# The last expert layer's end: gate multiplied into the down weights, the second tile summed by TensorE, the output stored in halves

## The reference

```python
def post_norm(x, y, gate, g, b):
    return layer_norm(DEEPNORM_ALPHA * x + gate * y, g, b)
...
    combine = jnp.sum(jax.nn.one_hot(e_idx, N_EXPERTS, dtype=jnp.float32) * wts[..., None], -2)
    hid = jax.nn.silu(jnp.einsum('bld,edf->blef', h, w_gate)) * jnp.einsum('bld,edf->blef', h, w_up)
    y = jnp.einsum('blef,efd->bld', hid * combine[..., None].astype(hid.dtype), w_down)
...
        x = post_norm(x, moe(modulate(x, ml[3], ml[4]), w_router, b_router, w_gate[i], w_up[i], w_down[i]),
                      ml[5], ln_g[i, 1], ln_b[i, 1])
```

## Time and profile before

| what | value |
|---|---|
| median of 3 runs | 901.22 us (898.92 to 905.03) |
| the profiled execution | 900.66 us |
| its span in the trace | 898.8 us |
| TensorE busy | 740.8 us (82% of the span) |
| VectorE busy | 477.4 us (53%) |
| DMA share and rate, 825 to 850 us | 1.02, 404 GB/s |
| TensorE busy from 870 us to the end | 0 us |

### The profile page before, as it was taken

One profiled execution on the slowest core, in us unless ns is written; L12 is line 12 of the kernel. 1 busy time (PEld: TensorE's weight loads), 2 busy tenths in 40 slices (PEclk: granted clock), 3 DMA queues, 4 the chain that ended last, 5 costly groups with the idle time before them and its releaser, 6 DMA issues. The chain is left out here.

```text
span 898.8 us, 15497 instructions
## 1 busy us (share of the span) xinstructions
PE 740.8 (82%) x5225; PEld 431.1 (48%) x5225; DVE 477.4 (53%) x1089; ACT 316.9 (35%) x778; POOL 300.1 (33%) x702
## 2 busy tenths in 40 slices
PE   0988879999997177999999999999898547999950
PEld 0544435555553023556666566665655233555520
DVE  1048654533334583643767777777744753443326
ACT  0240322222222225644657566575641121222211
POOL 0000113443344000366164846648440012434330
PEclk9989969999999569995999999999997857999985
DMA  9999999999990899576152442522110299999912
GB/s 250 408 394 393 411 412 406 408 408 346 359 390 25 326 367 261 186 205 209 41 145 52 108 124 53 142 60 100 43 60 1 104 403 392 404 405 407 376 65 112
DMA packets 107239, 219.34 MB, mean 244 GB/s; under 512 B 28293, under 2 KB 63437, under 8 KB 102817
## 3 DMA queue, kind: packets, MB, share of 16 engines
q1 hardware_dynamic: 98207, 200.39, 61.9%
q0 software_dynamic: 8224, 15.76, 4.6%
q10 hardware_dynamic: 740, 2.32, 0.9%
HBM read 212.09 MB, written 17.33 MB: 255 GB/s over the span
## 5 line engine op out<-in xcount | busy, mean ns | idle before, releaser
L1234 PE MATMUL banks<-h_cols,weight_ring 128*128 128x512 f32 (+1 forms) x384 | 160.3, 538 | 0.7
L1211 POOL TENSOR_TENSOR arena<-arena 128x60 f32<-128x60 f32 (+24 forms) x248 | 81.8, 330 | 123.3 <-DMA arena<-blocks 104.5
L1213 POOL TENSOR_TENSOR arena<-arena 128x60 f32<-128x60 f32 (+24 forms) x248 | 84.0, 339 | 19.4
L903 POOL DMA_INDIRECT y_of_tokens<-arena,place_now x42 | 47.3, 1126 | 127.9 <-ACT arena L795 127.9
L747 PE MATMUL banks<-arena 128*64 128x512 f32 x352 | 85.2, 605 | 3.0 <-DVE arena L839 3.0
L1234 PEld LDWEIGHTS banks<-h_cols,weight_ring 128*128 128x128 f32 x384 | 66.2, 194 | 34.7 <-issue 31.7
L875 POOL DMA_INDIRECT arena<-h_of_tokens,row_now x50 | 53.1, 1063 | 80.7 <-DVE token_of_slot L715 35.3
L287 PE MATMUL banks<-weight_ring,c_cols 128*32 128x512 f32 x368 | 52.3, 687 | 29.3 <-DMA weight_ring<-in_w_mod_dram 29.3
L765 PE MATMUL banks<-weight_ring,arena 128*64 128x256 f32 x576 | 67.6, 388 | 0.9 <-DVE arena L827 0.9
L831 DVE TENSOR_TENSOR arena<-arena,banks 128x128 f32<-128x128 f32 x42 | 12.1, 288 | 102.8 <-ACT arena L800 102.8
L800 ACT ACTIVATE arena<-banks 128x128 f32<-128x128 f32 x42 | 11.7, 278 | 143.1 <-PE banks L765 143.1
(11 more groups left out here) (291 smaller groups left out, 1374.7 us busy)
## 6 DMA issues: line engine op xcount, KB each, us to landing
weight_ring<-in_w_mod_dram SPq DMA_DIRECT2D x46, 1024.0 KB, 9.9
weight_ring<-in_dn_w_in_dram SPq DMA_DIRECT2D x32, 512.0 KB, 7.0
weight_ring<-in_w_gate_dram SPq DMA_DIRECT2D x13, 1024.0 KB, 10.5
weight_ring<-in_w_up_dram SPq DMA_DIRECT2D x13, 1024.0 KB, 14.6
weight_ring<-in_w_down_dram SPq DMA_DIRECT2D x13, 1024.0 KB, 15.5
arena<-in_w_gate_dram SPq DMA_DIRECT2D x7, 1024.0 KB, 12.5
arena<-in_w_up_dram SPq DMA_DIRECT2D x7, 1024.0 KB, 14.6
arena<-in_w_down_dram SPq DMA_DIRECT2D x7, 1024.0 KB, 16.3
```

Source lines behind the costliest of these rows:

```text
L903: pool.indirect_dma_start(y_halves, bass.IndirectOffsetOnAxis(m.place_now[:, u:u + 1], 0), v.y_tile[u], None, bounds_check=last_row, oob_i ...
L1211: then(pool.tensor_tensor(part, U[:, 0:q, j:j + 1].to_broadcast([P, q, BLK - 1 - j]), M[:, j, j + 1:BLK].unsqueeze(1).to_broadcast([P, q, ...
L1213: ins = pool.tensor_tensor(U[:, 0:q, j + 1:BLK], U[:, 0:q, j + 1:BLK], part, ALU.subtract)
L1234: mm = pe.matmul(bank(6 + j % 2)[:, 0:CTX + SEQ - n0], head_w[h % 2][:, j, k, :], m.hT[:, k, n0:CTX + SEQ], start=(k == 0), stop=(k == KD ...
```

## The change

- In the second layer, L839's copy becomes a product: `down_now` = down weights times the gate vector. In the first layer it stays a copy.
- Behind experts 2 and 3 VectorE multiplies one tile of x by ALPHA, in place; behind expert 4 it makes two diagonal matrices of 128 x 128 with the second tile's two weights (`weight_diag`).
- In GpSimd's loop (`pair`, in both layers) the wait for the earlier y store and the `place_now` copy stand first, ahead of `row_now` and the fetch of rows.
- Behind the last `down()` TensorE puts the second tile's x into banks 3 and 4 by a product with the identity (2 calls), makes 12 products into bank 1 that nobody reads, waits for the second tile's y and adds both pieces through the diagonals (4 calls).
- VectorE sums the first tile in two instructions instead of three, takes the second tile from the banks, and makes the last pass in halves of 512 columns. ScalarE no longer scales y.
- SyncE stores each half when it is done: four stores of 256 KB instead of two of 512 KB.

```diff
@@ dve_moe, tile
                 for to, of in down_pieces(expert_slot(L, e)):
-                    ins = dve.tensor_copy(to, of)
+                    if L.n == 0:
+                        ins = dve.tensor_copy(to, of)
+                    else:
+                        to, of = (x.rearrange("p (c n) -> p c n", n=D) for x in (to, of))
+                        ins = dve.tensor_tensor(to, of, mod_vec(GATE2).unsqueeze(1).to_broadcast([P, to.shape[1], D]), ALU.mult)
                 ins.then_inc(s(t_ + "hidden"), 1)
@@ dve_moe, behind expert e
+                if L.n == 1 and 2 <= e < 2 + XT:
+                    dve.wait_ge(s("ln_x"), MT + 2 * XT)
+                    x = m.x[:, L.x_tiles[e - 2], :]
+                    dve.tensor_scalar(x, x, ALPHA, None, ALU.mult).then_inc(s("x_scaled"), 1)
+                if L.n == 1 and e == 2 + XT:
+                    for c in range(2):
+                        dve.tensor_scalar(weight_diag[c], v.ident, v.weights[:, c, 1:2], None, ALU.mult).then_inc(s("x_scaled"), 1)
@@ pool_moe, pair
                 for u in range(2):
+                    if not first:
+                        pool.wait_ge(s(t_ + f"y_stored{u}"), 16 * j - 16)
+                    pool.tensor_copy(m.place_now[:, u:u + 1], m.place_of[:, bass.ds(2 * j + u - 2, 1)]
+                                     ).then_inc(s(t_ + f"place_now{u}"), 1)
                     pool.wait_ge(s(t_ + "rows_copied"), 2 * j + u + 1)
...
                     rows(u, u)
-                    if not first:
-                        pool.wait_ge(s(t_ + f"y_stored{u}"), 16 * j - 16)
-                    pool.tensor_copy(m.place_now[:, u:u + 1], m.place_of[:, bass.ds(2 * j + u - 2, 1)]
-                                     ).then_inc(s(t_ + f"place_now{u}"), 1)
@@ new
+        def pe_last_sum(pe):
+            t = XT - 1
+            pe.wait_ge(s("x_scaled"), XT + 2)
+            for half in range(2):
+                pe.matmul(m.ps[:, 3 + half, :], v.ident, m.x[:, L1.x_tiles[t], half * BANK:(half + 1) * BANK], start=True, stop=False)
+            for n in range(12):
+                pe.matmul(m.ps[:, 1, :], v.ident, m.const[:, 0:BANK], start=True, stop=True)
+            pe.wait_ge(s(f"y_back{t % 2}"), 32 * 3)
+            for c in range(2):
+                for half in range(2):
+                    mm = pe.matmul(m.ps[:, 3 + half, :], weight_diag[c], v.back[:, t, c, half * BANK:(half + 1) * BANK],
+                                   start=False, stop=(c == 1))
+            mm.then_inc(s("y_mixed"), 1)
+
+        def dve_last_norm(dve, t):
...
+            if t < XT - 1:
+                dve.wait_ge(s("x_scaled"), XT)
+                dve.wait_ge(s(f"y_back{t % 2}"), 32 * 3)
+                dve.scalar_tensor_tensor(out=x, in0=v.back[:, t, 0, :], scalar=v.weights[:, 0, t:t + 1], in1=x, op0=ALU.mult,
+                                         op1=ALU.add).then_inc(s("ln_gated"), 1)
+                dve.wait_ge(s("ln_gated"), c + 1)
+                dve.scalar_tensor_tensor(out=x, in0=v.back[:, t, 1, :], scalar=v.weights[:, 1, t:t + 1], in1=x, op0=ALU.mult,
+                                         op1=ALU.add).then_inc(s("ln_summed"), 1)
+                dve.wait_ge(s("ln_summed"), c + 1)
+            else:
+                dve.wait_ge(s("y_mixed"), MT + 1)
+                x = last_sum()
@@ sync
             for n, t in enumerate(L1.x_tiles):
-                sp.wait_ge(s("ln_x"), MT + 2 * XT + n + 1)
-                sp.dma_start(out_dram[0, n * P:(n + 1) * P, :], m.x[:, t, :]).then_inc(s("stored"), 16)
-            sp.wait_ge(s("stored"), 16 * XT)
+                for half in range(2):
+                    cols = slice(half * BANK, (half + 1) * BANK)
+                    sp.wait_ge(s("ln_x"), MT + 2 * XT + 2 * n + half + 1)
+                    sp.dma_start(out_dram[0, n * P:(n + 1) * P, cols], m.x[:, t, cols]).then_inc(s("stored"), 16)
+            sp.wait_ge(s("stored"), 16 * XT * 2)
@@ tensor
             pe_moe(pe, L1)
+            pe_last_sum(pe)
```

More of the change, by code:

```diff
@@ L924, in sp_back, with last_sum @@
                     sp.dma_start(v.back[:, t, c, :], y_dram[row:row + P, :]).then_inc(s(f"y_back{t % 2}"), 16)
+        weight_diag = [m.c_cols.rearrange("p k n -> p (k n)")[:, c * P:(c + 1) * P] for c in range(2)]
+        def last_sum():
+            return m.ps[:, 3:5, :].rearrange("p a n -> p (a n)")
+        def pe_last_sum(pe):
[11 more added lines that the diff above has]
+            mm.then_inc(s("y_mixed"), 1)
@@ new lines, in dve_last_norm @@
+        def dve_last_norm(dve, t):
+            c = LN_BASE["ln1b_"] + t
+            x = m.x[:, L1.x_tiles[t], :]
+            if t < XT - 1:
[11 more added lines that the diff above has]
+            for half in range(2):
+                dve.bn_stats(v.stats[:, 2 * (t % 2) + half, :], x[:, half * BANK:(half + 1) * BANK]).then_inc(s("ln_stats"), 1)
+            dve.wait_ge(s("ln_stats"), 2 * c + 2)
+            dve.bn_aggr(v.mean_var[:, t, 0:2], v.stats[:, 2 * (t % 2):2 * (t % 2) + 2, :]).then_inc(s("ln_var"), 1)
@@ new lines, in dve_last_centred @@
+        def dve_last_centred(dve, t):
+            c = LN_BASE["ln1b_"] + t
+            x = m.x[:, L1.x_tiles[t], :]
+            dve.wait_ge(s("ln_var"), c + 1)
+            dve.scalar_tensor_tensor(out=x, in0=x if t < XT - 1 else last_sum(), scalar=v.mean_var[:, t, 0:1], in1=m.ln[:, 0, :],
+                                     op0=ALU.subtract, op1=ALU.mult).then_inc(s("ln_centred"), 1)
+            dve.wait_ge(s("ln_std"), c + 1)
+            dve.reciprocal(v.mean_var[:, t, 2:3], v.std[:, t:t + 1]).then_inc(s("ln_rstd"), 1)
@@ L926, in act_back, with dve_last_scaled @@
+        def dve_last_scaled(dve, t, half):
+            c = LN_BASE["ln1b_"] + t
+            cols = slice(half * BANK, (half + 1) * BANK)
+            x = m.x[:, L1.x_tiles[t], cols]
+            dve.wait_ge(s("ln_centred"), c + 1)
+            dve.wait_ge(s("ln_rstd"), c + 1)
+            dve.scalar_tensor_tensor(out=x, in0=x, scalar=v.mean_var[:, t, 2:3], in1=m.ln[:, 1, cols], op0=ALU.mult, op1=ALU.add
+                                     ).then_inc(s("ln_x"), 1)
         def act_back(act, L, t):
@@ L2200, in _ @@
             act_moe(act, L1)
-            act_moe_norms(act, L1, "ln1b_")
+            for t in range(XT):
+                act_std(act, "ln1b_", t)
         @block.tensor
@@ L2328, in _ @@
             for t in range(XT):
[L2329 to L2332, removed]
+                dve_last_norm(dve, t)
+                dve_last_centred(dve, t)
+                for half in range(2):
+                    dve_last_scaled(dve, t, half)
 def constants():
```

## The result

The changed kernel takes 897.06 us (median of 9 runs, 894.75 to 899.06), the one before 901.53 us (9 runs, 898.92 to 907.34): ratio 0.9941, 95% interval 0.9917 to 0.9965. By the medians that is 4.5 us less, or 0.5%; by the ratio it is 0.6%, 5.3 us. 893.5 was forecast, 7.7 us less. The profiled execution has a span of 897.2 us; at 899.06 us it is the longest of the nine.

What follows compares the result with a forecast made beforehand. Bound: TensorE in the loop, then the chain from last down product to last store. 0.04 + 5.95 + 0.65 at the end plus 1.1 in the first layer make 7.7 us less: 893.5 us, range 890.5 to 897.5.

Steps and rivals of the forecast that it cites:

- (b): Rival: TensorE's clock falls in the longer gap before the last down product, +2 to +3.5 us, 896 us; chance 0.08.
- The product: Second layer's loop, VectorE: down weights times gate take 2.30 us against the copy's 1.22, 1.08 us more per tile.
- Its cover in the loop: The 1.08 us fit VectorE's idle time before L831 (2.50, tightest 1.18) and cost nothing, except at the last tile.
- VectorE's two tiles: End of the kernel: first tile 7.01 us instead of 8.07, second 4.45 us; together with the earlier start, -5.95 us.
- TensorE's sum: Behind the loop: TensorE's adding of the second y, done at 885.0, is hidden behind VectorE's first tile by 0.3 us.
- The half store: End of the kernel: the last store carries 256 KB instead of 512, 0.65 us less; bounds nothing and 0.65.
- GpSimd's order in the second layer: Last y_out no longer waits for the place_now copy; gain spent on the longer product, -0.04 us left.
- The first layer's 1.1 us: End of the first layer: GpSimd's new order sends the y store 1.4 to 0.9 us earlier, 1.1 taken.
- (a): Rival: behind the first layer the weight stream sets the end, so that layer's gain is lost, 894.6 us; chance 0.1.
- (c): Rival: VectorE's last products hold GpSimd up, last y store 0.2 to 0.7 us late, 894 us; chance 0.06.
- (d): Rival: behind the loop the unread products don't keep 2.4 GHz, some 10 us slower; chance 0.04.
- (e): Rival: later releases of down slots starve the loop's weight stream, +7 us, about 900 us; chance 0.04.

Runs made afterwards that it cites:

- e2: The changed kernel, unchanged, run again: ratio 0.9931 to the kernel before.
- e5: The changed kernel without the twelve products that nobody reads: ratio 0.9952 to the kernel before.
- e3: The kernel before with only GpSimd's new order, the copy of places ahead of the fetch, in both layers: ratio 0.9978 to the kernel before.
- e12: Repeat of e6, the changed kernel with the product of the down weights in two instructions: 894.58 us, ratio 0.9903 to the kernel before.
- e13: The changed kernel, unchanged, a third time, on one chip with e12: 896.37 us, ratio 0.9913 to the kernel before.
- e8: The changed kernel with each tile's last pass whole again and two stores of 512 KB: ratio 0.9923 to the kernel before.
- e1: The kernel before, unchanged, run again: ratio 1.0002.
- e6: The changed kernel with the product of the down weights in two instructions of 1024 values: ratio 0.9915 to the kernel before.

## Why the prediction was right, and where its size was off

*How close it was.* The gain is under one per cent, the case that was given a chance of 0.67. But 897.06 us lie 3.6 over the forecast and only 0.4 inside the range, and luck has a part in that. The range reached up to 897.5 through the spread of runs, through rival (b), and through a slip in the sum: the terms named for its lower bound give 0.04 + 5.95 - 0.3 + 0.9 = 6.6 us, not 5.9, and with 6.6 the 2 us of spread would have ended it at 896.6. That the first profile bears out every step at the end is luck too, as the repeats show: it is the one of eight in which the clock held.

*Right, by their own numbers.* The product: 2.30 us forecast, 2.28 in the profile. Its cover in the loop: the loop is as long as before, to 0.01 us. x times ALPHA: 0.68 us, in idle time. VectorE's two tiles: 7.01 and 4.45 forecast, 7.00 and 4.44. TensorE's sum: hidden, by 0.3 us as forecast, by 0.55 in the first profile and by 0.1 in e2; and the unread products do what was said (e5). The half store: 0.65 forecast, 3.1 to 2.45 measured. GpSimd's order in the second layer: its gain of 1.2 to 1.3 us (e3) pays for the longer product, 0.04 us left forecast, 4.45 to 4.32 us from the start of the last copy or product to y_out measured. With a clock that holds, the end is 6.7 us shorter where 6.6 were forecast.

*Mis-sized, too small.* The first layer's 1.1 us, with 0.9 to 1.4 as bounds, measured 1.5 on average (B, 1.4 to 1.8 for the kernels with the new order against those without, e12 and e13 1.2 to 1.5). The sum took 0.6 us from the end of GpSimd's fetch to the y store, the middle of its 0.30 to 0.80, and 0.31 stand there; the fetch beside VectorE's passes started 0.12 us earlier than forecast and took 1.24 us this time, not 1.36.

*Mis-sized, too large, the main one: the clock at the last down product.* The sum took 1.94 us for it and put the fall of the clock among the rivals, (b), with a chance of 0.08. Of eight profiles with 2.58 us of idle time there, seven have 2.7 to 3.2 us, and of six with 1.5 us none is slow. The split product, which keeps the work and takes only the idle time away, takes the slow product away with it. So the likely end is 5.4 us shorter, not 6.6, and 28.65 us stand where 27.4 were expected.

The evidence against (b) was weak. The row at 0.50 that spoke for it stands behind an idle time of 2.64 us in the same trace, about as long as the new one:

```profile
701.86 0.44 PE L1700 MATMUL banks<-const,arena 128*128 128x128 f32 x2 [2.64 <-DVE arena L1690]
702.87 8.83 PE L1717 MATMUL banks<-weight_ring,modulation 128*128 128x512 f32 x16 [0.56 <-ACT modulation L1705]
```

The clock falls behind it in 13 of the 14 profiles of this study, all but e8's. The row that spoke against (b), 354 to 357 at 1.00, holds most of an idle time of 3.25 us, and that it kept its clock was the exception: in this idle time or right behind it the clock falls in 11 of the 14 profiles, and the first one of the kernel before is one of the other three. In e1, the same program again, the stretches (columns: us, PE busy, TensorE clock, DMA share, GB/s) read:

```profile
355.00:358.00 3.00, 0.33 (x1) 1.00 0.23 81
359.00:362.00 3.00, 3.00 (x13) 0.50 0.90 289
```

One execution was too little to set a chance by. (b)'s price, on the other hand, was too high: +2 to +3.5 us were given and the profiles have 1.2 to 1.3. Only a part of the down product ran at 1.2 GHz (in e2 the clock was still 0.69 on average from 870 to 871), so it took 0.8 to 1.2 us more and not 1.94; and the clock was back within the first products behind it, whose delay stayed hidden, if barely (in e2 TensorE's sum ends at 889.06 and VectorE is free at 889.15).

*The rest.* 1.5 in the first layer and 5.4 at the end are 6.9 us. Three measurements gave 4.5, 6.2 and 6.7 by medians; by their ratios they gave 5.3, 6.2 and 7.9, with intervals of 3.2 to 7.5, 4.4 to 8.1 and 5.8 to 9.9. All three hold 6.9 and two hold 7.7, so the times can't tell the forecast's sum from the mended one; the profiles do. The stages ahead add a spread of their own. From VectorE's first instruction on the first layer's y to the second layer's first L831, where the instructions are the same, the kernel before took 453.2 and 454.9 us and the changed one 457.2, 455.3 and 455.0; the ten profiles with a new end average 454.4 and the other four 454.2. Of the 5.1 us by which the first changed profile stood late at the last product, 4.0 come from this stretch. The longer A in eight profiles of ten may belong to the change, about 1 us on average; that isn't settled.

*The other rivals.* (a) is out: B's gain is there in all profiles with the new order, and e3's ratio has it. (c) happened as a mechanism and cost nothing: the y store beside the product took 2.17 us instead of 1.12, and the last y store still followed y_out's end by 0.80 us, as before. (d) and (e) are out: the unread products ran at 1.00, and the loop is as long as before.

## What to carry to other kernels

Work moved from the path into covered time has one place where the cover ends, here the last tile behind the loop; look there for the longer instruction's full price, and try to split it there so that the waiting engine starts on the first half. A longer wait of TensorE costs more than its length if the clock falls behind it: look up what stood ahead of every row at half clock, and ask more than one execution before a chance is set. Products that nobody reads can be worth their place: here 12 of them were worth 2.6 us, and without them the move to TensorE gained nothing.

## What the runs showed of the hardware

- After 2.58 us of idle time behind a full loop the granted clock fell to 0.50 during the next product in seven profiles of eight, and not in the eighth; after 1.5 us it didn't in any of six, nor at the first layer's end, where all fourteen profiles have 1.5 us of idle time and 1.94 us for the down product. At two other places it fell behind 2.64 us in 13 profiles of 14 and in or right behind 3.25 us in 11 of 14, with both outcomes in the two executions of the kernel before. The eighth profile also differs at the loop's start, 110 us earlier: its first 32 records of L765 took 6.63 us, those of the other seven 5.1 to 5.6. Whether the two belong together stays open.
- A VectorE product with two SBUF inputs holds back GpSimd's indirect store: the store that began at 870.85 beside a product until 872.12 ended 0.90 us behind it. In that profile, the first of the changed kernel, all 13 stores of the second layer beside a product of 2048 values took 2.15 to 2.24 us, the four beside two products of 1024 values 1.09 to 1.11, and the last one, alone, 1.01. In e12, where all products are in two, all 17 took 1.09 to 1.17. The one at 865.74 in the kernel before, beside a copy until 865.95, ended 0.91 behind that the earlier trace rows, so a copy seems to do the same. The Trainium skill, SBUF — State Buffer, section "SBUF: two separate sides", has the lock that one of the two holds for a whole instruction; the trace agrees, 2.17 us against 1.01 alone, and a store gets in between two products.
- A store of 256 KB landed 2.0 us behind its issue and one of 512 KB 2.6 us (the changed kernel and e8).
- Two executions of one program differ by 1.1 us in a stage of 52 us, by the moment at which the clock comes back (e6 and e12), and three executions of the changed kernel by 2.2 us in a stretch of 455 us.
